# Latent input projections as 2x2 block products in Strassen's scheme, on one Trainium2 core

## The chip, the cores and the metric

The kernel runs on one core of a Trainium2 chip. The metric is the device time of one execution in microseconds (us); the number given for a kernel is the median of its runs. Engines are named as in the profile: PE is TensorE (PEld its weight loads), DVE is VectorE, ACT is ScalarE, POOL is GpSimd, SP is SyncE, whose queue issues the transfers.

## What is computed

One layer of a diffusion trunk for 128 context tokens and 1024 latent tokens of width 1024, all in float32. What matters here is the combined input projection, whose columns feed a pooling mixer, eight DeltaNet heads (q, k, v and gate, 128 columns each) and two merge gates:

```python
h = rmsnorm(x, norm1_g) * (1 + scale1) + shift1
proj = h @ w_in
a_out = pool_mixer(proj[..., OFF_POOL:OFF_Q], pool_w, pool_scale, grid) @ pool_proj
b_in, s_f, s_b = deltanet_mixer(proj, dn_conv, dn_a_log, dn_dt_bias, dn_onorm_g, s0_f, s0_b)
b_out = b_in @ dn_proj
merge = jax.nn.sigmoid(proj[..., OFF_MERGE:])
mixed = merge[..., :D_MODEL] * a_out + merge[..., D_MODEL:] * b_out
x = x + gate1 * (mixed @ w_out)
h = rmsnorm(x, norm2_g) * (1 + scale2) + shift2
x = x + gate2 * expert_choice_ffn(h, router_w, exp_w_gate, exp_w_up, exp_w_down)
```

`deltanet_mixer` applies a short convolution of five taps to q, k and v, normalises q and k, and runs a gated delta rule in chunks in both directions. `expert_choice_ffn` is a mixture of 16 experts; the change does not touch it.

## The kernel before, in words

The prologue computes the modulation, normalises and turns x into `hT3` (128 partitions x 8 steps of the contraction x 1152 tokens, context first) and makes q, k and v of head 0. Then a loop runs over heads 0 to 6 and a second copy of its body does head 7. After that come the merge of the branches, the output projection, the routing and the experts.

**Projections are the filling of the head loop.** A unit of work is one tile of 128 output columns over one span of tokens (span 0 is the 128 context tokens, spans 1 and 2 are 512 latent tokens each): `KD` = 8 matmuls that accumulate in one of PSUM banks 6 and 7, which alternate (`project`, L616). ACT copies each finished unit out (`evac_unit`, L647). One head's body projects q, k, v for the next head, the gate `g` of its own and two "side" tiles `A` and `B` of the merge and pooling columns, 18 units in the order `ORDER`; the last head does `g` and the side tiles A to F (`ORDER_LAST`). A unit may start when the unit two places before it has been copied out (`pj_drained`). The matmuls of the units are cut into pieces by the table `FILLS`, and `fill(place)` puts each piece between two dependent steps of the head's own work, so that PE has something to do while the others answer.

**The head's own work, in order of its places:** the norm of k ("nk", L765, which waits for ACT's silu and squares), q turned ("qT", L770), k and v turned (L779), the products kk and kq ("kk", L787). DVE multiplies kk with the decay table `dm` (L1085), which POOL has masked before (L1232), forms the first triangles (L1092, L1097), and PE turns them ("Y20" to "Y22", L794). Six levels double the size of the inverted blocks: products Z and P on PE (L802), copies on ACT (L976, L979), and on DVE nine predicated copies in each level (L1111, L1118, L1123) and one tap of the next head's convolution (L1053, L1055). Then "res", "fix" and the scan over nine chunks ("scan1a" to "scan8c"). POOL takes four differences and products of 1152 columns during the levels (L1247, L1250) and, when the scan has ended, adds and squares both directions' outputs (L1253, L1255); DVE and ACT normalise them (L1188, L1029, L1190), ACT does the silu of the gate (L1035), PE turns the result (L895), and DVE's last steps release the next head (`scan_done`). The fills "end1" and "end2" stand between the scan and that turning.

SP's queue, in the order of `head`: weights of q, v, k two heads on when `k2` is done, the next gate's weights, side tile A out and its next weights in, then the decay rows and states, side tile B out and its next weights in.

```python
ins = nc.tensor.matmul(unit_bank(order, name)[:, 0:n], w[:, k, :], hT3[:, k, at:at + n], start=(k == 0), stop=(k == KD - 1))
```

## Time and profile before

| | |
|---|---|
| median of 3 runs | 2492.16 us (2490.82 to 2493.74) |
| span of the profiled execution | 2491.1 us |
| around the span (median less span) | 1.1 us |
| PE, PEld busy | 96%, 70% of the span |
| DVE, ACT, POOL busy | 40%, 38%, 11% |
| one head of the loop | 140.6 us |
| matmuls of the projections (L616) | 925.2 us of 2401.1 us of PE |

An instruction of the profile has a line of the source, an engine, and the tiles it reads and writes; here nearly all tiles are views of one buffer, `arena`, so that lines tell more than names. A float32 matmul stands in the profile as two instructions. Durations of neighbouring matmuls overlap, so that a run of them is read from its start and end and not from the mean of one.

### The profile page before, as it was taken

The numbers are of one execution on the slowest core, as the hardware profiler recorded it, in microseconds if no ns is written. First come the engines' busy times: TensorE is split into PE (matmuls) and PEld (weight loads), VectorE is DVE, ScalarE is ACT, GpSimd is POOL, SyncE is SP. The second block draws the span as 40 slices with busy tenths as digits, with TensorE's granted clock in tenths as the row PEclk, the third lists the DMA queues.
The fourth block names the chain that finished last, engine by engine and source line by source line (L and its number), as shares of the span: only waits on it lengthen the run. The fifth ranks groups of instructions, "written<-read, shape, count | busy, mean of one in ns | idle before, by whom it ended". The sixth has DMA issues, their size and how long they took to land.

```text
span 2491.1 us, 39690 instructions
## 1 busy us (share of the span) xinstructions
PE 2401.1 (96%) x14448; PEld 1732.1 (70%) x14448; DVE 1007.9 (40%) x2061; ACT 938.0 (38%) x2447; POOL 285.9 (11%) x193
## 2 busy tenths in 40 slices
PE   6999999999999999999999999959999999999998
PEld 3466656566666656565644444649999999999996
DVE  2567575747556575744424524740001000100013
ACT  3164645556374655545421123212322232223213
POOL 0021221203111221201000000000101010101000
PEclk8999999999999999999999999979999999999999
DMA  9511212120201212021342422358886888688864
GB/s 335 221 48 37 68 37 68 26 79 1 76 29 37 68 37 68 1 78 37 107 178 106 146 75 93 119 178 279 287 298 232 288 286 299 230 287 287 299 230 160
DMA packets 198455, 361.94 MB, mean 145 GB/s; under 512 B 8954, under 2 KB 72327, under 8 KB 195243
## 3 DMA queue, kind: packets, MB, share of 16 engines
q1 hardware_dynamic: 192139, 341.77, 39.3%
q0 software_dynamic: 6176, 18.29, 2.9%
q8 instruction: 90, 1.47, 0.3%
q14 instruction: 50, 0.41, 0.1%
HBM read 319.97 MB, written 40.06 MB: 145 GB/s over the span
## 4 chain that ended last, share of the span: by engine, by line
PE 93%; DVE 2%; DMA 1%; issue 1%; ACT 1%; SPq 0%; DVEq 0%; POOL 0%; ACTq 0%; POOLq 0%
PE bank L616 32%; PE bank L2139 20%; PE bank L2153 10%; PE bank L1768 5%; PE bank L1505 4%; PE bank L802 3%; PE bank L1523 2%; PE bank L794 2%; PE bank L871 1%; PE bank L860 1%; PE bank L876 1%; PE bank L787 1%; DMA arena<-in_ada_w 1%; PE bank L851 1%; PE bank L875 1%
## 5 line engine op out<-in xcount | busy, mean ns | idle before, releaser
L616 PE MATMUL bank<-arena 128*128 128x512 f32 (+1 forms) x2496 | 925.2, 496 | 2.9 <-issue 1.2
L2139 PE MATMUL bank<-arena 128*128 128x144 f32 x4096 | 513.0, 286 | 3.0 <-ACT arena L2187 3.0
L2139 PEld LDWEIGHTS bank<-arena 128*128 128x128 f32 x4096 | 509.7, 190 | 3.2 <-ACT arena L2187 3.2
L616 PEld LDWEIGHTS bank<-arena 128*128 128x128 f32 x2496 | 374.6, 192 | 156.4 <-issue 154.0
L2254 DVE TENSOR_TENSOR arena<-arena,bank 128x144 f32<-128x144 f32 x128 | 39.2, 306 | 700.0 <-ACT arena L2201 700.0
L2153 PE MATMUL bank<-arena 128*128 128x144 f32 x2048 | 257.3, 286 | 0.7 <-DVE arena L2254 0.7
L2153 PEld LDWEIGHTS bank<-arena 128*128 128x128 f32 x2048 | 253.8, 190 | 1.9 <-DVE arena L2254 0.9
L802 PEld LDWEIGHTS bank<-arena 128*128 128x128 f16 x1296 | 98.3, 98 | 169.2 <-issue 156.1
L976 ACT ACTIVATE arena<-bank 128x384 f16<-128x384 f16 (+1 forms) x360 | 160.0, 495 | 140.1 <-PE bank L802 102.0
L2201 ACT ACTIVATE arena<-bank 128x144 f32<-128x144 f32 x128 | 37.4, 292 | 464.3 <-PE bank L2139 464.3
L647 ACT ACTIVATE arena<-bank 128x512 f32<-128x512 f32 (+1 forms) x156 | 76.6, 491 | 253.3 <-PE bank L616 253.0
L1055 DVE SCALAR_TENSOR_TENSOR arena<-arena 128x1156 f32<-128x1156 f32 x96 | 136.2, 1419 | 1.6 <-issue 1.3
L1768 PE MATMUL bank<-arena 128*128 128x512 f32 x288 | 128.7, 601 | 4.1 <-DVE arena L1662 2.1
L1111 DVE CAST_PREDICATED arena<-arena,bank 128x384 f16<-128x384 uint32 x144 | 79.8, 554 | 119.3 <-PE bank L802 119.1
L802 PE MATMUL bank<-arena 128*128 128x128 f16 x1296 | 123.7, 220 | 0.7 <-ACT arena L976 0.3
L1505 PE MATMUL bank<-arena 128*128 128x512 f32 x256 | 110.6, 592 | 1.3 <-DVE arena L1202 1.3
L1118 DVE COPY_PREDICATED arena<-arena 128x384 f16<-128x384 uint32 x144 | 101.1, 702 | 7.0 <-ACT arena L979 0.9
L1768 PEld LDWEIGHTS bank<-arena 128*128 128x128 f32 x288 | 53.9, 192 | 68.5 <-issue 66.3
L2208 ACT ACTIVATE arena<-bank,arena 128x128 f32<-128x128 f32 x128 | 47.2, 368 | 135.9 <-PE bank L2153 135.9
L1009 ACT ACTIVATE arena<-bank,arena 128x128 f32<-128x128 f32 x144 | 53.3, 370 | 106.1 <-PE bank L860 106.1
L1505 PEld LDWEIGHTS bank<-arena 128*128 128x128 f32 x256 | 48.4, 189 | 62.5 <-issue 60.9
L1168 DVE SCALAR_TENSOR_TENSOR arena<-arena,bank 128x128 f32<-128x128 f32 x128 | 44.7, 349 | 98.0 <-PE bank L876 98.0
(296 smaller groups left out, 2733.8 us busy)
## 6 DMA issues: line engine op xcount, KB each, us to landing
arena<-in_exp_w_gate SPq DMA_DIRECT2D x32, 2048.0 KB, 10.0
arena<-in_exp_w_up SPq DMA_DIRECT2D x32, 2048.0 KB, 15.0
arena<-in_exp_w_down SPq DMA_DIRECT2D x32, 2048.0 KB, 11.0
arena<-in_w_in SPq DMA_DIRECT2D x52, 512.0 KB, 5.3
arena<-in_ada_w SPq DMA_DIRECT2D x24, 1024.0 KB, 7.9
side_dram<-arena SPq DMA_DIRECT2D x20, 576.0 KB, 3.3
arena<-g_dram SPq DMA_DIRECT2D x16, 576.0 KB, 4.9
arena<-in_x_sample SPq DMA_DIRECT2D x16, 512.0 KB, 7.3
```

Of the source, the lines that this page charges most:

```text
L616: ins = nc.tensor.matmul(unit_bank(order, name)[:, 0:n], w[:, k, :], hT3[:, k, at:at + n], start=(k == 0), stop=(k == KD - 1))
L647: nc.scalar.activation(dst, bank[:, 0:n], ACT.Copy).then_inc(sem("pj_drained"), 1)
L802: last = nc.tensor.matmul(TRI[d][g][:, i * P:(i + 1) * P], lhs[:, 3 * g + i, :], rhs[:, 3 * g + i, :], start=(n == 0), stop=(n == len(term ...
L976: nc.scalar.activation(flat(dst, g), src[:, 0:384], ACT.Copy).then_inc(sem(f"drained{d}_act"), 1)
L1009: nc.scalar.activation(scan[:, 2, d, :], TRI[d][1][:, 0:P], ACT.Copy, scale=tab["kd"][:, ti, bass.ds(h + d * H, 1)])
L1055: ins = nc.vector.scalar_tensor_tensor(conv_to[j][:, 0:CW], raw[j][:, tap:tap + CW], w, conv_to[j][:, 0:CW], ALU.mult, ALU.add)
L1111: nc.vector.copy_predicated(up[:, 3 * g:3 * g + 3, :], masks[:, 0, lv + 1, :].unsqueeze(1).to_broadcast([P, 3, P]), TRI[1][g][:, 0:384].re ...
L1118: nc.vector.copy_predicated(low[:, 3 * g:3 * g + 3, :], rows, up[:, 3 * g:3 * g + 3, :]).then_inc(sem("low_changed"), 1)
L1505: last = nc.tensor.matmul(banks[n % RING][:, 0:CH], w_dn[half][:, k, col:col + P], bT3[:, k, CTX + c * CH:CTX + (c + 1) * CH], start=(k == ...
L1768: last = nc.tensor.matmul(banks[2 * (i % 2) + half][:, 0:512], mixT3[:, k, t * P:(t + 1) * P], w_outs[:, k, half * 512:(half + 1) * 512], ...
L2139: last = nc.tensor.matmul(banks[3 + f % 2][:, m * CAP:(m + 1) * CAP], w_unit[2 * half + m][:, k, col:col + P], xsT[:, k, :], start=(k == 0 ...
L2153: last = nc.tensor.matmul(banks[5 + dt % 2][:, 0:CAP], w_unit[4 + half][:, k, col:col + P], hid[:, k, :], start=(k == 0), stop=(k == KD - 1))
```

## The change

The latent tokens are two halves of 512 (`LH`), the contraction is two halves of 4 steps (`KH`), and the tiles of the loop are taken in pairs: (q,v), (k,g), (A,B), in the last head (A,B), (C,D), (E,F), with the last head's `g` alone. For a pair the latent part is a product of 2x2 blocks. It is done in seven block products of 4 matmuls of 512 columns, in place of eight; the jobs are called `1`, `2`, `6`, `7`, `5`, `4`, `3`, and the context units `c0` and `c1` go first. Four of the seven take sums of weight blocks or of blocks of x.

- The sums of x (three of 128x2048, and one in place over a block of `hT3`) are made once by POOL in the prologue. The last head's g2 therefore uses sums of weights too.
- The sums of weights (four of 128x512 for a pair, twelve in a head) are made by POOL in each head, in `sums_first` (two), `sums_third` and `sums_fourth`, the third once `c1` is done, the fourth once `2` is done.
- Jobs 6, 5, 3 accumulate on the bank of job 1, and 4 on that of job 7. Jobs `1`, `6`, `7`, `3` and the context are copied out by ACT, as many copies as before; jobs `2`, `5`, `4` are added to a result by DVE (`add_job`), nine adds of 128x512 from PSUM in a head, at places named by `add(place)`. A job waits for the copy or add of the job two before it, and the first job of a head for all of them.
- The table of pieces counts columns (`FILL`, units of 512) in place of matmuls. "start" has 5 units where it had 6 matmuls; "end1" has 4 where it had 6, "end2" 5 where it had 8.
- Side tiles A and B are both stored, and their next weights both loaded, after the head's last job. `w_dn` is loaded later; some buffers move, `attnT` shares `dm`.

```diff
+        PAIR_JOBS = ("c0", "c1", "1", "2", "6", "7", "5", "4", "3")
-        ORDER = ("q1", "q0", "v0", "k0", "g0", "A0", "B0", "q2", "v1", "v2", "k1", "k2", "g1", "g2", "A1", "A2", "B1", "B2")
-        ORDER_LAST = ("g1", "g0", "A0", "B0", "g2", "A1", "A2", "B1", "B2") + tuple(f"{x}{i}" for x in "CDEF" for i in range(3))
+        ORDER = pair_jobs("qv") + pair_jobs("kg") + pair_jobs("AB")
+        ORDER_LAST = pair_jobs("AB") + ("g0", "g1", "g2") + pair_jobs("CD") + pair_jobs("EF")
-        FILLS = {"start": 6, "nk": 5, "qT": 16, "kk": 16, "Y20": 8, "Y21": 8, "Y22": 2, "X0": 1, "X1": 1, "X2": 1, "res": 2, "fix": 4, "end1": 6}
+        UNIT = 512
+        FILL = {"start": 5, "nk": 2.75, "qT": 4, "kk": 4, "Y20": 1.5, "Y21": 1.5, "Y22": 1, "X0": 1, "X1": 1, "X2": 1, "res": 2, "fix": 3, "end1": 4}
+        def project(pe, h, order):
+            for i, job in enumerate(order):
+                bank = job_bank(order, job)
+                if i >= 2:
+                    bank_read(pe, h, order, order[i - 2])
+                elif order is not FIRST:
+                    pe.wait_ge(sem("pj_drained"), len(FIRST) + N_COPIES * h)
+                    pe.wait_ge(sem("pj_added"), 1 + N_SUMS * h)
...
+                else:
+                    one, two = weights_of(job[0]), weights_of(job[1])
+                    w, x = {"1": (one[:, 0:KH, :], h11), "2": (one[:, KH:KD, :], h21), "6": (w_sum[1], h_sum2), "7": (two[:, 0:KH, :], h_sum3),
+                            "5": (w_sum[0], h_sum1), "4": (two[:, KH:KD, :], h_sum4), "3": (one[:, KH:KD, :], h22)}[job[2]]
+                    if job[2] in "6573":
+                        pe.wait_ge(sem("sums_ready"), sums_before(h, order, job) + {"5": 1, "6": 2, "7": 3, "3": 4}[job[2]])
+                    for k in range(KH):
+                        ins = nc.tensor.matmul(bank[:, 0:LH], w[:, k, :], x[:, k, :], start=(k == 0 and job[2] in "127"), stop=(k == KH - 1), skip_group_check=(job[2] in "6543"))
...
+        def add_job(dve, h, order, job):
+
+            name, span, copied = {"2": (job[0], 1, "1"), "5": (job[1], 2, "7"), "4": (job[1], 1, "6")}[job[2]]
+            dve.wait_ge(sem("pj_drained"), copied_at(h, order, job[:2] + copied))
+            dve.wait_ge(sem("pj_filled"), job_at(h, order, job))
+            to = result(h, order, name, span)
+            nc.vector.tensor_tensor(to, to, job_bank(order, job)[:, 0:LH], ALU.add).then_inc(sem("pj_added"), 1)
...
+            def sums_first(pair, used):
+
+                n = sums_before(h, order, pair)
+                for name in pair:
+                    weights_wait(pool, h, order, name)
+                pool.wait_ge(sem("pj_filled"), used)
+                one, two = weights_of(pair[0]), weights_of(pair[1])
+                nc.gpsimd.tensor_tensor(w_sum[0], two[:, 0:KH, :], two[:, KH:KD, :], ALU.add).then_inc(sem("sums_ready"), 1)
+                summed(n + 1)
+                nc.gpsimd.tensor_tensor(w_sum[1], w_sum[0], one[:, 0:KH, :], ALU.subtract).then_inc(sem("sums_ready"), 1)
...
+            def sums_fourth(pair):
+
+                one = weights_of(pair[0])
+                pool.wait_ge(sem("pj_filled"), job_at(h, order, pair + "2"))
+                summed(sums_before(h, order, pair) + 2)
+                nc.gpsimd.tensor_tensor(one[:, KH:KD, :], one[:, KH:KD, :], w_sum[1], ALU.subtract).then_inc(sem("sums_ready"), 1)
...
+            first, second, third = ("AB", "CD", "EF") if last_h else ("qv", "kg", "AB")
+            pool.wait_ge(sem("scan_done"), h + 1)
+            sums_first(first, len(FIRST) + len(ORDER) * h)
+            sums_third(first)
+            sums_fourth(first)
```

In the rows below a line stands for its line in the kernel concerned: in the changed kernel L729 and L718 are the block and context matmuls, L1392 to L1407 the sums of weights, L1427 the masking of `dm` (L1232 before), L911 the products kk and kq (L787 before), L918 the turning for Y2 (L794 before).

**POOL, the loop's body from its start to the mask of Yf, before:**

```order
L1389 UNCONDITIONAL_BRANCH
L1389 ISA
L1232 ISA [waits decay_exp]
L1232 AFFINE_SELECT arena<-arena 128x1152
L1230 REGISTER_ALU
L1232 AFFINE_SELECT arena<-arena 128x1152 [waits decay_exp]
L1237 ISA
L1239 AFFINE_SELECT arena<-arena 128x384 [waits X_init] x6
```

and in the changed kernel:

```order
L1392 TENSOR_TENSOR arena<-arena 128x512 [waits pj_filled]
L1383 ISA
L1394 TENSOR_TENSOR arena<-arena 128x512 [waits sums_ready]
L1399 REGISTER_ALU
L1400 TENSOR_TENSOR arena<-arena 128x512 [waits pj_filled]
L1405 REGISTER_ALU
L1383 REGISTER_ALU [waits pj_filled]
L1407 TENSOR_TENSOR arena<-arena 128x512 [waits sums_ready]
L1425 ISA
L1427 ISA [waits decay_exp]
L1427 AFFINE_SELECT arena<-arena 128x1152
```

The four sums of the pair (q,v) stand ahead of the two masks of `dm`, and the last of them (L1407) waits for the job `2` of the pair.

**PE in the same body, from the end of kk and kq to the first turning for Y2, before:**

```order
L787 MATMUL bank<-arena 128x128 x2
L616 MATMUL bank<-arena 128x128 x5
L608 REGISTER_ALU
L614 REGISTER_ALU [waits w_in3]
L616 MATMUL bank<-arena 128x128 [waits pj_drained]
L616 MATMUL bank<-arena 128x128 x7
L614 REGISTER_ALU [waits w_side_in0]
L616 MATMUL bank<-arena 128x128 [waits pj_drained]
L616 MATMUL bank<-arena 128x128 x2
L807 ISA
L544 ISA [waits X_init]
```

and in the changed kernel, where the single L729 is the last matmul of job `qv2`, the next four are `qv6`, and the one that waits for `pj_added` is the first of `qv7`:

```order
L911 MATMUL bank<-arena 128x128 x2
L729 MATMUL bank<-arena 128x512
L668 REGISTER_ALU
L727 ISA [waits pj_drained]
L729 MATMUL bank<-arena 128x512 [waits sums_ready]
L729 MATMUL bank<-arena 128x512 x2
L931 ISA
L556 REGISTER_ALU [waits X_init]
...
L729 MATMUL bank<-arena 128x512
L666 REGISTER_ALU
L727 REGISTER_ALU [waits pj_added]
L729 MATMUL bank<-arena 128x512 [waits sums_ready]
```

The last matmul of `qv2` stands behind kk and kq, and `qv7` stands between the first and the second turning.

**SP, the last body's transfers between the head before it and its own, changed kernel:**

```order
L797 DMA arena<-g_dram 128x1152
L799 DMA arena<-in_state_dn_bwd 128x128
L788 DMA side_dram<-arena 128x1152 [waits pj_drained,pj_added]
L779 DMA arena<-in_w_in 128x8x128
L788 DMA side_dram<-arena 128x1152 [waits pj_drained,pj_added]
L779 DMA arena<-in_w_in 128x8x128
```

The last head begins with the pair (A,B), whose weights are the two L779; they are issued when the jobs of the head before have been copied and added. Before, the last head began with `g`, whose weights came much earlier.

## Rows read from the trace of the kernel before

**Rows 1.** The page: busy time of PE, and its granted clock in 40 slices.
```profile
PE 2401.1 (96%) x14448; PEld 1732.1 (70%) x14448; DVE 1007.9 (40%) x2061; ACT 938.0 (38%) x2447; POOL 285.9 (11%) x193
PEclk8999999999999999999999999979999999999999
```

**Rows 2.** Groups by line and shape, PE: busy us, mean ns; idle before.
```profile
L616 PE MATMUL bank<-arena 128*128 128x512 f32 x1664 | 821.4, 604 | 2.3 <-issue 1.2 <-ACT arena L287 1.0
```

**Rows 3.** The chain that ended last, in order of time: start us, us, what.
```profile
1098.96 12.88 PE bank L616 x30
...
1275.76 27.74 PE bank L1505 x64
```

**Rows 4.** Timeline of PE, head 1 to head 2: start us, us, engine, line.
```profile
395.55 13.04 PE L616 MATMUL bank<-arena 128*128 128x512 f32 x30
408.43 1.15 PE L895 MATMUL bank<-arena 128*128 128x128 f32 x9
...
414.91 2.10 PE L765 MATMUL bank<-arena 128*128 128x128 f32 x6
...
425.83 4.18 PE L787 MATMUL bank<-arena 128*128 128x128 f32 x36
429.85 3.74 PE L616 MATMUL bank<-arena 128*128 128x128 f32 x32
433.65 0.51 PE L794 MATMUL bank<-arena 128*128 128x128 f16 x6
...
442.03 0.34 PE L802 MATMUL bank<-arena 128*128 128x128 f16 x3
```

**Rows 5.** Timeline of POOL, same stretch.
```profile
426.95 2.37 POOL L1232 TENSOR_SCALAR_AFFINE_SELECT arena<-arena 128x1152 f32<-128x1152 f32 x2 [24.74 <-ACT arena L958]
```

**Rows 6.** Timeline of DVE: prologue's end, same stretch, merge.
```profile
128.10 0.06 DVE L1224 MEMSET arena<- 128x1 f32 x1
...
404.20 1.36 DVE L1190 TENSOR_TENSOR arena<-arena 128x1152 f32<-128x1152 f32 x1 [0.61 <-ACT arena L1031]
...
432.49 2.91 DVE L1097 COPY_PREDICATED arena<-arena 128x384 f16<-128x384 uint32 x6
...
1283.00 0.69 DVE L1564 TENSOR_TENSOR arena<-arena,bank 128x512 f32<-128x512 f32 x1 [1.99 <-PE bank L1505]
```

**Rows 7.** Timeline of ACT, same stretch.
```profile
405.48 1.26 ACT L1035 ACTIVATE arena<-arena 128x128 f32<-128x128 f32 x2
408.63 0.60 ACT L647 ACTIVATE arena<-bank 128x512 f32<-128x512 f32 x1 [1.89 <-PE bank L616]
...
416.69 1.52 ACT L935 ACTIVATE arena<-bank,arena 128x128 f32<-128x128 f32 x3
...
425.52 2.23 ACT L958 ACTIVATE arena<-arena 128x1152 f32<-128x1152 f32 x2
```

**Rows 8.** Windows: us, then busy of PE, PEld, DVE, ACT, POOL, clock, DMA.
```profile
416.69:422.88 6.19, 6.19 (x44) 5.07 (x43) 3.22 (x11) 6.09 (x26) 0.00 (x0) 1.00 0.00 0
```

**Rows 9.** Timeline of POOL, in the levels and in the last head.
```profile
339.30 3.73 POOL L1250 TENSOR_TENSOR arena<-arena 128x1152 f32<-128x1152 f32 x1 [4.01 <-DVE arena L1123]
...
1245.60 2.62 POOL L1253 TENSOR_TENSOR arena<-arena 128x1152 f32<-128x1152 f32 x1 [47.57 <-ACT arena L1015]
```

**Rows 10.** Timeline of DVE in the levels: predicated copies, alone and beside POOL.
```profile
309.51 0.56 DVE L1123 COPY_PREDICATED arena<-arena 128x384 f16<-128x384 uint32 x1
...
341.63 1.82 DVE L1118 COPY_PREDICATED arena<-arena 128x384 f16<-128x384 uint32 x1
```

**Rows 11.** Timeline of PE: behind a pause in the first head, and in the levels.
```profile
132.24 3.56 PE L765 MATMUL bank<-arena 128*128 128x128 f32 x6 [2.79 <-ACT arena L923]
...
310.75 0.33 PE L794 MATMUL bank<-arena 128*128 128x128 f16 x3
```

**Rows 12.** Windows, the same pause's end (columns as in rows 8).
```profile
132.00:134.00 2.00, 1.76 (x4) 1.27 (x5) 1.54 (x8) 2.00 (x5) 0.00 (x0) 0.50 1.16 295
```

**Rows 13.** Transfers of heads by tensor: queue, count, KB each, us to landing.
```profile
arena<-in_w_in SPq DMA_DIRECT2D x46, 512.0 KB, 5.1
```

More of the change, by code:

```diff
@@ L754, in body_pe @@
             order = ORDER_LAST if last_h else ORDER
-            side_work = projections(pe, h, order)
+            side_work = project(pe, h, order)
             def fill(place):
-                for _ in range(FILLS.get(place, UNITS_MAX * KD)):
-                    next(side_work, None)
+                for _ in range(steps_of(order, place)):
+                    next(side_work)
             fill("start")
@@ L907, in evac @@
             def evac(place):
-                for name in units_of(order, place):
-                    evac_unit(act, h, order, name)
+                for job in jobs_of(order, place):
+                    if not is_sum(job):
+                        copy_job(act, h, order, job)
             def silu(j):
@@ L1058, in body_dve, with add @@
         def body_dve(dve, h, last_h=False):
+            order = ORDER_LAST if last_h else ORDER
+            added = [0]
+            def add(place):
+                to = jobs_until(order, place)
+                for job in order[added[0]:to]:
+                    if is_sum(job):
+                        add_job(dve, h, order, job)
+                added[0] = to
             def decay_arguments(d):
@@ L1072, in body_dve @@
             decay_arguments(1)
+            add("qT")
             for g in range(3):
@@ L1150, in body_dve @@
             dve.wait_ge(sem("attn_ready"), 2 * h + 2)
+            add("fix")
             def remainder(t):
@@ L1179, in body_dve @@
             tap()
+            add("scan1b")
             state(1)
@@ L1183, in body_dve @@
                 tap()
+                add(f"scan{t}b")
                 state(t)
```

370 lines of the change are left out of this document (255 added, 115 removed).

## The prediction

> **What bounds the kernel now.** I read the page first: PE is busy for 96% of the span and its clock is granted in full nearly everywhere [rows 1]. The groups by line and shape then say what PE does: the 512-column matmuls of the projections alone are 821 us in 1664 instructions [rows 2]. The chain in order of time gives the pace: the fill behind the scan starts at 395.55 and again at 1098.96 us, five heads later, so a head takes 140.7 us [rows 3, 4], and within it PE hardly pauses. So fewer matmuls are worth their time, but only where the next dependent step is ready when PE arrives. That is a question for the timelines of the other engines. I count time in a head from 395.55 us, where the fill behind the last scan step begins [rows 4].
>
> **What the change takes off PE.** 30 instructions, that is 15 matmuls of 512 columns, last 12.88 us [rows 3, 4]: 0.86 us each. Each pair of tiles needs 28 in place of 32, and there are three pairs in each of eight heads: 96 matmuls, 82.4 us, 10.3 us a head. The context columns stay as many. This is the whole gain on offer. By the tables of pieces, of one head's 12 units (of 512 columns) 5 go behind the scan, 1.75 before kk, 4.25 among the turnings for Y2 and 1 at "fix"; none goes in the levels.
>
> **Behind the scan.** PE has 10 matmuls left in place of 15: 8.6 us. But the normalised output that the turning L895 needs is ready only when DVE's L1190 ends, at 404.20 + 1.36 = 405.56, that is 10.0 [rows 6]; before, PE came to it at 12.9 and was itself the last. So PE waits 1.4 us; L895 takes 1.2 to the next matmul (to 409.66), until 11.2. New: the next head's first job waits for the copy of job `AB3`, which ACT makes only after the silu of the gate, ended at 406.74, 11.2 [rows 7], 0.6 us more: 11.8. From the end of such a copy (409.23) to ACT's norms (416.69) are 7.5 us [rows 7]; so they come at 19.3, and with two context copies in front of them at 19.8, where it was 21.1. ACT is now the last here. Its work to the end of q's norm is 6.2 us less one copy of 0.5 [rows 8], then the copy of `qv1` (0.6) and the first of k turned (0.5): kk starts at 26.6, where it was 30.3 (425.83), and ends at 30.6 [rows 4]. So 3.7 us of the 5.8 that the smaller fills leave have been gained up to here.
>
> **The step that gives it back.** POOL's fourth sum stands ahead of the masks of `dm` and waits for job `2`, whose last matmul stands behind kk and kq: done at 31.5. A sum of 512 columns I price by POOL's add of 1152 alone, 2.62 us [rows 9]: 1.2 us. So the masks start at 32.8; they were at 426.95, 31.4 [rows 5]. From the mask to the first turning for Y2 (433.65) are 6.7 us of DVE and POOL [rows 4, 5]: 39.5, where it was 38.1. PE has `qv6` to do until 34.1 and then stands still for 5.4 us. Next, `qv7` needs the add of `qv2`, which DVE makes behind the six L1097: they end 1.75 us after the first turning starts [rows 4, 6], and the add, priced by a DVE product of 512 columns from PSUM, takes 0.69 [rows 6]. PE comes at 40.7 and waits until 41.9. Three of its matmuls and two turnings of 0.35 later, at 45.2, the levels begin; they began at 46.5 (442.03) [rows 4]. Of 9.5 us of matmuls saved up to here 1.3 are left.
>
> **The clock.** In the first head PE stood idle for 2.79 us, and the norm's matmuls behind it took 3.56 us at a granted clock of 0.50, the lower of its two levels (1.2 GHz), where they take 2.10 at the full one [rows 4, 11, 12]. 5.4 us idle will do the same: up to 1.5 us lost, of which the wait for the add hides half: 0.8. So the levels start 0.5 earlier than before.
>
> **The levels.** POOL's sums for (k,g) fall here. Beside POOL's product of 1152 a predicated copy of DVE lasts 1.82 us, alone 0.56, and POOL's product takes 3.73 where the add alone takes 2.62 [rows 9, 10]: they stop each other. And a copy that ends at 310.07 is turned by PE at 310.75, in the next level [rows 10, 11]: about 0.7 us of slack. Two sums back to back (behind `qv5`, in the first level) move DVE by up to 1.65 us: 1.15 lost; the third and fourth, one sum each, 0.65 and 0.8; the first two for (A,B) fall on the last copies before "res": 1.0. Together 3.6, less the matmul saved at "fix": 2.75. DVE's own adds fit into its waits. The bounds are nothing (each sum meets DVE in a wait) and the full 1.16 us for all eight sums from the levels on, 9.3 us. I take a value in the lower part, as each sum has slack in front of it. The Trainium skill, "SBUF — State Buffer", section "Who interferes with whom", says that a VectorE instruction with two SBUF inputs and a GpSimd one that reads SBUF exclude each other for a whole instruction; were none of it absorbed, the upper bound would hold. That is the fourth rival.
>
> **The scan.** The same columns, but "scan2b" has a context matmul of 128 where 512 stood, so that PE waits about 0.65 for ACT, and 0.2 for DVE's taps beside two sums: 0.85.
>
> **A head of the loop:** -1.3 + 0.8 + 2.75 + 0.85 = +3.1 us.
>
> **The ends.** The first fill must now wait for DVE's prologue (128.1 [rows 6], where PE had started at 124): with 4.5 us of jobs and about 1 us of delay by POOL's sums of x (4.7 us each by rows 9) its norm starts at 133.7, not 132.2 [rows 11]: +1.5, and 0.8 of clock. The last head had 10.6 units in front of Y2 and twice 4 in it, so there PE was the last; with masks, add and POOL's sums at the same distances its levels start at 48.6 in place of 61, then 8 more matmuls in the scan and 18 fewer behind it, and 2 us for sums, make it 9.9 us shorter from the scan of head 6 to L1505 (it lasted 1275.76 - 1098.96 = 176.8 [rows 3]). But its first job now needs the weights of A, issued after 11.8 and 5.1 us under way [rows 13], 0.4 for a store and issue ahead: 17.9, and B's at 18.8; this puts it back by 5.9, with 1.5 and 0.8 of clock: -1.7.
>
> **The sum:** 2.3 for the first front, six rounds from levels to levels 18.6, the rest of head 6 3.6, the last head -1.7: +22.8. The profiled execution took 2491.1 us of span and 1.1 around it, the median; so 2515 us.
>
> **Rivals.** (1) *PE stays the last everywhere* and the 82 us are gained, less the 5.9 of the last head: 2416. For it: PE's 96%. Against: L1190, the masks and the add have fixed distances that the removed fills covered. Chance 0.06. (2) *POOL's sums leave DVE alone*, since each falls into a wait. Then the levels give back nothing and a head is -1.3 + 0.8 - 0.86 + 0.65 = -0.7; with 2.3 for the front, -0.2 for the rest of head 6 and -3.7 for the last head the sum is -5.8: 2486, and 2479 if the clock stays full. DVE's waits of about 1 us in a level speak for it, the copy of 1.82 us against. Chance 0.17. (3) *The masks are not late*, the case on the other side. Masks that start when the first exponential of `dm` is done (28.5, L958 behind the copies of k [rows 7]) let Y2 turn at 35.3; PE waits 1.2 us only and keeps its clock, and the levels start 4.2 + 0.8 us sooner. A head is then -1.9 and eight of them take 40 us off my sum: 2475, with light sums as in (2) down to 2445. It decides from the point where job `2` ends before that exponential, 3 us earlier than I have it. Against it stands the order, with job `2` behind kk. Chance 0.15. (4) *DVE becomes the bound of the levels*: 9.3 us in place of 3.6, in eight heads +46: 2561. Chance 0.07. That the change doesn't do what it says I exclude for the matmuls; their number is fixed.
>
> **Numbers.** My case has 0.55. It reaches from 2500 to 2530, as each of the walk's nine waits may be off by some tenths and is taken seven times. Down to 2470 the range takes in rivals 2 and the greater part of 3; above it ends at 2535. Outside are 1 and 4 and a little of my own. 0.2%, about what a measurement of this kernel can tell, is 5 us. Faster by more: rivals 1, 3 and half of 2, 0.29; within: the rest of 2 and a little of mine, 0.13; slower: 0.58.
>
> **What would show it.** L729 and L718 together near 843 us in 2304 instructions. A pause of PE of about 5 us in front of L918 in each head, put down to DVE or POOL, and a clock below 1 there; L1407 of the first pair just ahead of L1427; a second pause before `qv7`; 1 to 2 us in front of L895's successor; predicated copies of DVE above 1 us more often than three times a head. I am wrong if PE reaches the levels more than 3 us earlier in a head than before (the masks did not count), or if the levels last 42 us as now (the sums did not count).

## The result, and the profile after

The changed kernel is slower: 2571.47 us (2571.28 to 2572.18, 4 runs) against 2492.95 us (2490.82 to 2494.79, 4 runs) on the same chip, a ratio of 1.0318 with a 95% interval of 1.0303 to 1.0333. The prediction was 2515 us with a range up to 2535: the sign was right, the size was not. The span of the profiled execution is 2569.5 us, 78.4 more than before.

The page of the changed kernel, busy time of the engines and PE's granted clock in 40 slices (before: [rows 1]):

```profile
PE 2370.0 (92%) x14256; PEld 1718.9 (67%) x14256; DVE 1122.5 (44%) x2133; ACT 943.5 (37%) x2447; POOL 440.5 (17%) x295
PEclk8989999999999999998999999979999999999999
```

PE is busy 31 us less and the kernel is 78 us longer, so PE now stands still for about 110 us more; DVE is busy for 115 us more and POOL for 155. The groups by line and shape (before: [rows 2]) show that the products are as few as intended, and, in the last column, new waits:

```profile
L729 PE MATMUL bank<-arena 128*128 128x512 f32 x1344 | 697.4, 622 | 21.6 <-ACT arena L763 21.6
L718 PE MATMUL bank<-arena 128*128 128x128 f32 x768 | 113.0, 298 | 16.3 <-DMA arena<-in_w_in 10.5 <-ACT arena L763 3.8 <-DVEq L1575 2.0
```

With the 69.8 us in 192 instructions of L710, the units outside a pair, the projections are 2304 instructions, the number that the prediction gave, but 880.2 us in place of its 843: 45 us less than before, not 82. That fits the clock: a 512-column instruction of L729 takes 622 ns on average where L616 took 604, and the mean granted clock of the execution is 0.968, where executions of the kernel before have 0.982 to 0.987.

One head of the loop in PE's timeline, from the fill behind the scan at 419.67 to the first products of the levels (L926) and on to the next fill. It is to be read against [rows 4]:

```profile
419.67 8.76 PE L729 MATMUL bank<-arena 128*128 128x512 f32 x20
429.75 1.20 PE L1019 MATMUL bank<-arena 128*128 128x128 f32 x9 [1.32 <-DVE arena L1343]
431.58 5.46 PE L718 MATMUL bank<-arena 128*128 128x128 f32 x32 [0.63 <-ACT arena L763]
439.15 1.12 PE L729 MATMUL bank<-arena 128*128 128x512 f32 x2 [2.11 <-ACT arena L763]
440.11 2.10 PE L889 MATMUL bank<-arena 128*128 128x128 f32 x6
442.05 1.88 PE L729 MATMUL bank<-arena 128*128 128x512 f32 x4
443.77 1.15 PE L894 MATMUL bank<-arena 128*128 128x128 f32 x9
444.75 3.60 PE L729 MATMUL bank<-arena 128*128 128x512 f32 x8
448.19 2.13 PE L903 MATMUL bank<-arena 128*128 128x128 f32 x18
450.15 4.18 PE L911 MATMUL bank<-arena 128*128 128x128 f32 x36
454.17 3.60 PE L729 MATMUL bank<-arena 128*128 128x512 f32 x8
463.36 0.82 PE L918 MATMUL bank<-arena 128*128 128x128 f16 x6 [5.59 <-DVE arena L1242]
463.97 3.93 PE L729 MATMUL bank<-arena 128*128 128x512 f32 x4
...
471.03 0.33 PE L926 MATMUL bank<-arena 128*128 128x128 f16 x3
...
569.21 8.76 PE L729 MATMUL bank<-arena 128*128 128x512 f32 x20
```

The head lasts 149.54 us where it lasted 140.6. Two pauses stand out: 2.11 us ahead of job `1`, which waits for ACT, and 5.59 us ahead of the first turning for Y2 (L918). From 439.15 to 457.7 PE does not pause at all.

The same places, read from the starts of these rows in each kernel, are used from here on. The times are us from the start of the fill behind the scan, the mean of the six rounds that lie within the loop; "scan" is the first matmul of the scan with the inverted blocks (L984 in the changed kernel), and the last column is the length of a head:

| kernel | norm (L889) | kk (L911) | Y2 (L918) | levels (L926) | scan | next fill |
|---|---|---|---|---|---|---|
| before | 19.5 | 30.4 | 38.2 | 46.6 | 102.05 | 140.6 |
| changed | 20.8 | 31.3 | 44.5 | 51.9 | 110.8 | 150.1 |
| fourth sum behind the masks | 20.75 | 31.45 | 40.4 | 46.3 | 105.1 | 144.5 |
| copy of c0 early | 16.7 | 26.8 | 40.0 | 46.9 | 105.8 | 145.1 |
| both | 16.7 | 26.8 | 35.7 | 41.6 | 100.5 | 139.8 |
| thin sums in the levels | 20.8 | 31.3 | 44.5 | 52.0 | 107.4 | 146.75 |
| thin adds | 21.0 | 31.6 | 44.8 | 52.0 | 110.8 | 150.2 |
| sums in quarters | 20.9 | 32.3 | 45.95 | 53.2 | 110.2 | 149.5 |
| before, less matmuls | 16.3 | 28.3 | 36.1 | 41.1 | 95.7 | 134.2 |
| five moves | 16.7 | 26.8 | 35.7 | 40.3 | 99.15 | 138.4 |
| and quarters | 16.7 | 26.8 | 35.6 | 40.25 | 97.2 | 136.5 |

POOL and ACT in that head name what is late. POOL's timeline (before: [rows 5]):

```profile
437.12 1.33 POOL L1400 TENSOR_TENSOR arena<-arena 128x512 f32<-128x512 f32 x1 [1.33 <-PE bank L718]
455.36 1.27 POOL L1407 TENSOR_TENSOR arena<-arena 128x512 f32<-128x512 f32 x1 [16.90 <-PE bank L729]
456.66 2.37 POOL L1427 TENSOR_SCALAR_AFFINE_SELECT arena<-arena 128x1152 f32<-128x1152 f32 x2
```

ACT's timeline, ahead of the norm (before: [rows 7]):

```profile
435.12 2.39 ACT L1040 ACTIVATE arena<-arena 128x128 f32<-128x128 f32 x4
437.52 1.28 ACT L1054 ACT_TABLE_LOAD   x1
438.82 0.45 ACT L763 ACTIVATE arena<-bank 128x128 f32<-128x128 f32 x2
```

The fourth sum (L1407) ends 0.03 us before the masks (L1427) start, and it has waited for job `2`, as the prediction had it. What the prediction had not seen is the last row: the copies of the two context jobs stand on ACT behind six silus (four of them in the first row) and a table load, although PE had c0 ready near 434, half way through its 32 context matmuls.

### The profile page after: what moved, and what is told of

It is laid out like the page before. It is cut to its first block, busy times and chain, and to the rows that moved or that the text cites. A ratio compares the mean times of both kernels' runs of the same rounds, so it can differ in the third digit from the quotient of the medians.

```text
span 2569.5 us, 39903 instructions
## 1 busy us (share of the span) xinstructions
PE 2370.0 (92%) x14256; PEld 1718.9 (67%) x14256; DVE 1122.5 (44%) x2133; ACT 943.5 (37%) x2447; POOL 440.5 (17%) x295
## 4 chain that ended last, share of the span: by engine, by line
PE 52%; DVE 2%; issue 1%; DMA 1%; ACT 1%; POOL 0%; SPq 0%; DVEq 0%; ACTq 0%; POOLq 0%
PE bank L2373 20%; PE bank L2387 10%; PE bank L2002 5%; PE bank L1739 4%; PE bank L729 3%; PE bank L1757 2%; PE bank L710 1%; PE bank L2011 1%; PE bank L2345 1%; PE bank L2355 1%; PE bank L926 0%; PE bank L718 0%; DMA arena<-in_w_in 0%; PE bank L2413 0%; PE bank L995 0%
## 5 line engine op out<-in xcount | busy, mean ns | idle before, releaser
L729 PE MATMUL bank<-arena 128*128 128x512 f32 x1344 | 697.4, 622 | 21.6 <-ACT arena L763 21.6
L2373 PEld LDWEIGHTS bank<-arena 128*128 128x128 f32 x4096 | 509.6, 190 | 3.2 <-ACT arena L2421 3.2
L729 PEld LDWEIGHTS bank<-arena 128*128 128x128 f32 x1344 | 221.9, 195 | 119.4 <-issue 95.0
L2387 PEld LDWEIGHTS bank<-arena 128*128 128x128 f32 x2048 | 253.8, 189 | 1.9 <-DVE arena L2488 0.9
L926 PEld LDWEIGHTS bank<-arena 128*128 128x128 f16 x1296 | 98.7, 98 | 149.8 <-issue 127.4
L1186 DVE SCALAR_TENSOR_TENSOR arena<-arena 128x1156 f32<-128x1156 f32 x96 | 143.1, 1490 | 0.3
L918 PE MATMUL bank<-arena 128*128 128x128 f16 x648 | 72.7, 233 | 70.8 <-DVE arena L1242 44.4
L2002 PE MATMUL bank<-arena 128*128 128x512 f32 x288 | 128.7, 601 | 4.1 <-DVE arena L1896 2.1
L718 PE MATMUL bank<-arena 128*128 128x128 f32 x768 | 113.0, 298 | 16.3 <-DMA arena<-in_w_in 10.5
L918 PEld LDWEIGHTS bank<-arena 128*128 128x128 f16 x648 | 46.5, 104 | 119.7 <-issue 65.7
L926 PE MATMUL bank<-arena 128*128 128x128 f16 x1296 | 123.5, 219 | 0.0
L718 PEld LDWEIGHTS bank<-arena 128*128 128x128 f32 x768 | 104.3, 210 | 26.3 <-issue 26.3
L763 ACT ACTIVATE arena<-bank 128x128 f32<-128x128 f32 (+1 forms) x156 | 76.1, 493 | 106.7 <-PE bank L710 48.0
L1264 DVE COPY_PREDICATED arena<-arena 128x384 f16<-128x384 uint32 x144 | 111.8, 776 | 6.8 <-DVE arena L1257 0.9
L1134 ACT ACTIVATE arena<-bank,arena 128x128 f32<-128x128 f32 x144 | 53.3, 370 | 165.0 <-PE bank L984 165.0
L1739 PE MATMUL bank<-arena 128*128 128x512 f32 x256 | 110.6, 592 | 1.3 <-DVE arena L1356 1.3
L1257 DVE CAST_PREDICATED arena<-arena,bank 128x384 f16<-128x384 uint32 x144 | 79.6, 552 | 65.9 <-PE bank L926 64.0
## 6 DMA issues: line engine op xcount, KB each, us to landing
arena<-in_exp_w_gate SPq DMA_DIRECT2D x32, 2048.0 KB, 10.1
```

The lines of the kernel that those rows point to most:

```text
L718: ins = nc.tensor.matmul(bank[:, 0:CTX], weights_of(name)[:, k, :], hT3[:, k, 0:CTX], start=(k == 0), stop=(k == KD - 1))
L729: ins = nc.tensor.matmul(bank[:, 0:LH], w[:, k, :], x[:, k, :], start=(k == 0 and job[2] in "127"), stop=(k == KH - 1), skip_group_check=( ...
L918: last = nc.tensor.transpose(TRI[d][g].bitcast(F16)[:, i * P:(i + 1) * P], src[:, 3 * g + i, :], ident_h)
L926: last = nc.tensor.matmul(TRI[d][g][:, i * P:(i + 1) * P], lhs[:, 3 * g + i, :], rhs[:, 3 * g + i, :], start=(n == 0), stop=(n == len(term ...
L1186: ins = nc.vector.scalar_tensor_tensor(conv_to[j][:, 0:CW], raw[j][:, tap:tap + CW], w, conv_to[j][:, 0:CW], ALU.mult, ALU.add)
L1257: nc.vector.copy_predicated(up[:, 3 * g:3 * g + 3, :], masks[:, 0, lv + 1, :].unsqueeze(1).to_broadcast([P, 3, P]), TRI[1][g][:, 0:384].re ...
```

## The experiments

A ratio is to the kernel before on the same chip as the experiment. The medians of that kernel there were 2493.24 to 2495.27 us, against 2492.95 beside the changed kernel, so differences to the changed kernel's 2571.47 us are good to about 2 us.

### The two pauses, each taken away alone

The first edit lets POOL make the fourth sum behind the masks of `dm` (and, in the last head, lets the gate's sums wait for it, not shown):

```diff
             sums_third(first)
-            sums_fourth(first)
             for d in range(2):
...
                 nc.gpsimd.affine_select(out=dm[d], in_=dm[d], ...)
+            sums_fourth(first)
```

> The changed kernel with one step moved: POOL makes the fourth sum of the first pair behind the two masks of dm and not ahead of them. Theory A (the masks are the step that is late, and the sum is what makes them late): the changed kernel's masks start 1.3 us behind job 2 (456.66 us), its first exponential of dm ends near 451, so DVE's first product with dm starts when PE's kk and ACT's exponential are there, near 452.6 in place of 458.0; Y2 turns 5.4 us earlier, PE's 5.6 us pause in front of it goes to under 0.5, and the stretch at a clock of 0.5 behind it (2.2 us lost) goes too, while the add of qv2 holds qv7 up by about 0.9. That is 5.4 to 7.4 us in each of eight heads: 2512 to 2528 us. Theory B (something else ahead of the levels is last, DVE's adds or the copies of ACT): at most the 1.3 us of one sum a head, 2561 or more.

Measured: 2531.51 us (2522.48 to 2540.09), 40 less than the changed kernel; ratio to before 1.0156 (1.0120 to 1.0191). From kk to Y2 it takes 8.9 us in place of 13.2, and the levels begin 5.9 us behind Y2 in place of 7.4. Theory A holds in kind, 3.5 us outside its numbers: Y2 comes 4.3 us sooner behind kk, not 5.4. DVE shows why. In one of its heads, kk being at 440.84:

```profile
443.31 2.88 DVE L1230 SCALAR_TENSOR_TENSOR arena<-bank,arena 128x384 f32<-128x384 f32 x6
446.10 2.57 DVE L1237 TENSOR_TENSOR arena<-arena 128x384 f16<-128x384 f32 x3
```

The three L1237 take 2.57 us where they took 1.49 in the changed kernel, because the moved sum runs at 446.05, beside them. The spread of 18 us has a likely cause of its own, told in the last section.

The second edit puts ACT's copy of c0 between the squares of k and the silu of q:

```diff
             silu(1)
+            act.wait_ge(sem("scan_done"), h + 1)
+            copy_job(act, h, order, order[0])
             silu(0)
             silu(2)
             act.preload_act_table_set(LN_EXP)
-            act.wait_ge(sem("scan_done"), h + 1)
-            evac("start")
+            for job in jobs_of(order, "start")[1:]:
+                copy_job(act, h, order, job)
```

> The changed kernel with ACT's copy of the first job (qvc0) put between the squares of k and the silu of q, in place of behind all six silus and the table load. Theory A (in front of the norm PE waits 2.1 us for that copy, and from the norm to kk PE is itself the last, so what is late there stays late): PE starts the norm of k 2.1 us sooner in each head, kk, the masks and Y2 follow by the same 2.1 us; 4 us in the first head; 2551 to 2556 us. Theory B (the pause is harmless, as ACT's norms and the transposes set the time of kk, as the prediction had it): under 0.7 us a head, 2566 or more.

Measured: 2540.22 us (2535.37 to 2541.23), 31 less; ratio to before 1.0183 (1.0166 to 1.0200). Theory A was right in kind but foresaw only half of the size: kk comes 4.5 us earlier, not 2.1. Its PE timeline:

```profile
420.12 3.83 PE L718 MATMUL bank<-arena 128*128 128x128 f32 x32 [0.63 <-ACT arena L763]
423.97 1.13 PE L729 MATMUL bank<-arena 128*128 128x512 f32 x2
424.93 2.10 PE L889 MATMUL bank<-arena 128*128 128x128 f32 x6
```

The 32 context matmuls take 3.83 us and not 5.46: the clock is full here. In the changed kernel some heads also have the 3.83 us, but there the time only made the pause for the copy longer (3.74 in place of 2.11).

Both edits together:

> The changed kernel with both moves: POOL's fourth sum of the first pair behind the masks, and ACT's copy of the first job in front of the silu of q. Theory A (two pauses of PE one behind the other, each on the path): the norm of k at 16.7 us of a head, kk 10.0 behind it, Y2 8.9 behind kk, the levels 5.9 behind that, the scan 58.9 and the next head 39.3 further: 139.8 us a head, where the changed kernel has 149.5 to 150.7; the last head like that of the first move alone. 2490 us. Theory B (the pauses overlap, so that the second move gives only what the first has left): 2515 us or more. A third possibility: the stretch of low clock behind a pause falls on the norm and the turnings in some heads, as with the first move alone, 2.9 us in each such head: 2493 to 2510.

Measured: 2495.22 us (2493.76 to 2498.93, 10 runs), ratio to before 1.0008 (0.9998 to 1.0018), no difference that can be measured. A head lasts 139.77 us, within 0.1 of theory A, though the whole is 5 us above its 2490; the low clock on the norm, by which the third possibility reached such times, is in none of the six rounds. So two places in the order of ACT and POOL made the whole loss against the kernel before, 76 us. In a round the edits gave 5.7 and 5.0 us one by one and 10.35 together, so they nearly add up. The medians gave 40 and 31; the first lies between two groups of runs 16 us apart, so that the 5 us missing to 76 say nothing.

### Sums and adds in the levels

Sums behind the first pair of a head were made of 1 column of each step, then all of DVE's adds of 1 column:

```diff
+                c = P if pair == first else 1
-                nc.gpsimd.tensor_tensor(w_sum[0], two[:, 0:KH, :], two[:, KH:KD, :], ALU.add).then_inc(sem("sums_ready"), 1)
+                nc.gpsimd.tensor_tensor(w_sum[0][:, :, 0:c], two[:, 0:KH, 0:c], two[:, KH:KD, 0:c], ALU.add).then_inc(sem("sums_ready"), 1)
...
```

```diff
-            nc.vector.tensor_tensor(to, to, job_bank(order, job)[:, 0:LH], ALU.add).then_inc(sem("pj_added"), 1)
+            nc.vector.tensor_tensor(to[:, 0:1], to[:, 0:1], job_bank(order, job)[:, 0:1], ALU.add).then_inc(sem("pj_added"), 1)
```

> The changed kernel with all sums of weights behind the first pair of a head made of 1 column in each of the four steps, where they have 128 (the products that use them are then not those of the reference). Theory A (POOL's sums and DVE's predicated copies keep each other out in the levels): the stretch from the first Z to the scan goes from 58.4 us to 54 or 55, 3.4 to 4.3 us a head of the loop, about 2541 to 2547 us. Theory B (the levels are longer because DVE also has nine adds to make): the stretch stays above 57.5 us, 2565 or more.

> The changed kernel with each of DVE's nine adds of a head made of 1 column where it has 512 (q, k, v, the gate and the side tiles are then not those of the reference). Theory A (the adds fall into DVE's waits, or behind Y2 where PE waits for one): under 1 us a head, 2563 to 2571 us. Theory B (the adds, 0.69 us each, stand on DVE's path in the levels and in the scan): 3 to 4 us a head, 2540 to 2547 us.

Measured: 2547.66 us (2545.85 to 2549.45) with thin sums, 2569.59 (2568.39 to 2572.10) with thin adds. The levels last 55.4 and 58.9 us, where the changed kernel has 58.9 and the kernel before 55.45. So the sums cost 3.4 us there, as much as the levels had grown, and the nine adds cost nothing there. The groups of DVE over the levels of one head, changed kernel (us busy, mean ns):

```profile
L1264 DVE COPY_PREDICATED arena<-arena 128x384 f16<-128x384 uint32 x18 | 14.4, 798 | 0.9 <-DVE arena L1257 0.2
L1269 DVE COPY_PREDICATED arena<-arena 128x384 f16<-128x384 uint32 x18 | 13.1, 728 | 0.9
L1257 DVE CAST_PREDICATED arena<-arena,bank 128x384 f16<-128x384 uint32 x18 | 9.9, 552 | 7.9 <-PE bank L926 7.9
L1186 DVE SCALAR_TENSOR_TENSOR arena<-arena 128x1156 f32<-128x1156 f32 x4 | 6.7, 1668 | 0.0
```

and with thin sums:

```profile
L1264 DVE COPY_PREDICATED arena<-arena 128x384 f16<-128x384 uint32 x18 | 13.3, 738 | 0.9 <-DVE arena L1257 0.2
L1269 DVE COPY_PREDICATED arena<-arena 128x384 f16<-128x384 uint32 x18 | 10.0, 558 | 0.9
L1257 DVE CAST_PREDICATED arena<-arena,bank 128x384 f16<-128x384 uint32 x18 | 9.9, 553 | 7.9 <-PE bank L926 7.9
L1186 DVE SCALAR_TENSOR_TENSOR arena<-arena 128x1156 f32<-128x1156 f32 x4 | 5.7, 1420 | 0.0
```

The predicated copies and taps with all inputs in SBUF lose 5.2 us to the sums (34.2 against 29.0), of which 3.4 are on the path; the one whose data come from PSUM (L1257) takes 552 ns beside a sum or not (all 144 of them 546 to 561 ns, one at 478.43 us in the middle of a sum that runs from 478.17 to 479.65). The Trainium skill, "SBUF — State Buffer", section "Who interferes with whom", has it so: outside the two-port modes a VectorE instruction with at most one SBUF input does not contend with GpSimd, while one with two contends with a GpSimd instruction that reads SBUF, over ports that only one of them holds at a time. The trace agrees, by the 552 ns on the one side and the 34.2 us against 29.0 on the other.

If a stall is as long as POOL's instruction, shorter instructions should help. Each sum as four:

```diff
+            def by_steps(out, one, two, op):
+                for k in range(KH):
+                    last = nc.gpsimd.tensor_tensor(out[:, k, :], one[:, k, :], two[:, k, :], op)
+                last.then_inc(sem("sums_ready"), 1)
...
-                nc.gpsimd.tensor_tensor(w_sum[0], two[:, 0:KH, :], two[:, KH:KD, :], ALU.add).then_inc(sem("sums_ready"), 1)
+                by_steps(w_sum[0], two[:, 0:KH, :], two[:, KH:KD, :], ALU.add)
```

> The changed kernel with each of the twelve sums of a head made by four instructions of 128 columns in place of one of 512. Theory A (POOL and DVE keep each other out for one whole instruction, so a shorter one of POOL holds a predicated copy up for less): the levels go from 58.9 us down to between 56 and 57.5; 2550 to 2562 us, if the four instructions take about as long as the one. Theory B (the two share in proportion to the time that POOL reads, whatever the length of its instructions): the levels stay at 58.9 or grow by the cost of more instructions; 2570 to 2590.

Measured: 2560.70 us (2558.88 to 2561.72), 11 less than the changed kernel, ratio to before 1.0268 (1.0251 to 1.0285). The levels last 57.0 us, as theory A has it. (kk is later here by the low clock, which more of the heads have, and Y2 by the fourth sum, whose four instructions stand ahead of the masks.) The predicated copies beside the first two sums of (k,g) took 1.63 and 1.17 us in the changed kernel; here three take 0.82, 0.76 and 0.81. That is so although POOL now needs 4.73 us for two sums that took some 2.9:

```profile
474.98 4.73 POOL L1387 TENSOR_TENSOR arena<-arena 128x128 f32<-128x128 f32 x8 [6.08 <-PE bank L729]
```

### Fewer matmuls and nothing else

In the kernel before, steps of the units were left out at about the places of the change:

```diff
+        SKIP = {"nk": 1, "qT": 3, "kk": 6, "Y20": 5, "Y21": 5, "Y22": 1, "fix": 1, "end1": 5}
+        SKIP_LAST = {"nk": 1, "kk": 2, "Y20": 2, "Y21": 1, "fix": 1, "end1": 5}
...
                 for k in range(KD):
+                    if order is not FIRST and 0 < k < KD - 1 and to_skip[0] > 0:
+                        to_skip[0] -= 1
+                        yield
+                        continue
```

> The kernel before with about as much matmul time left out as the change removes, at about the places where the change removes it (5 matmuls of 512 behind the scan, 1 and 3 of 128 before kk, 16 of 128 and 1 of 512 around Y2, 1 of 512 in fix; in the last head 12 of 512): 9.9 us a head, some 80 in all, and neither sums nor adds. Those units then lack one of eight steps. Theory A (the loss comes from the sums, the copies' place and the masks, and the saved time by itself is mostly worth having): the turning of o 2.8 us earlier, kk about 4, the levels 6.8 and the end of the head 7.6: 133 us a head, 2431 us, within 12. Theory B (PE is last everywhere): 80 us less, 2413. Theory C (the head is bound by the fixed chain of ACT, POOL and DVE, so that fewer matmuls give almost nothing even without the sums): 2475 to 2490.

Measured: 2441.21 us (2439.72 to 2442.21), ratio to before 0.9787 (0.9771 to 0.9804). The rounds give 6.4 us each of 9.9, 52 us of some 80 in all, inside theory A's range. Even with nothing added, then, a third of the saved time is lost: PE waits 1.3 us for DVE ahead of the turning of o, twice 1.1 us for ACT's copies ahead of kk, and 1.4 us for DVE ahead of Y2.

### What beats both

Three more moves on top of the two: DVE's add of `qv2` behind the first pair of L1242, the matmul of "scan8b" moved to the end of the head, and g0, g1 ahead of the pair (A,B) in the last head:

```diff
+                if g == 0:
+                    add("kk")
...
+        FILL[f"scan{NT - 1}b"] = 0
...
-        ORDER_LAST = pair_jobs("AB") + ("g0", "g1", "g2") + pair_jobs("CD") + pair_jobs("EF")
+        ORDER_LAST = ("g0", "g1") + pair_jobs("AB") + ("g2",) + pair_jobs("CD") + pair_jobs("EF")
```

> The two moves, and three more: DVE's add of qv2 stands behind the first pair of its six predicated copies for Y2, not behind all six; the matmul at scan8b goes to the end of the head, where PE waits 1.3 us; the last head begins with g0 and g1 and then takes the pair (A,B), whose weights come late. Theory A (each move takes away a wait of PE that is on the path): 1.05 us for the add in eight heads, 0.86 for the matmul in seven, about 5 for the last head, 19 us below the kernel with the two moves: 2471 us. Theory B (what is moved only turns up as the next wait): within 5 us of the kernel with the two moves, 2485 to 2495.

Measured: 2481.47 us (2478.85 to 2482.09), ratio to before 0.9946 (0.9929 to 0.9962), between the two theories. The rounds are 1.4 us shorter than with two moves: 1.3 from Y2 to the levels, so the add was on the path, but 0.1 in and behind the scan. The matmul at "scan8b" only made room for a wait of 0.5 for ACT. From the last scan of the loop to L1739's stage (L1745 here) it is 175.6 us, where it was 177.5: the weights of A are covered now, but PE waits ahead of Y2 for masks that stand behind the sums of that pair:

```profile
1129.91 0.39 PE L919 MATMUL bank<-arena 128*128 128x128 f16 x2 [6.97 <-DVE arena L1245]
```

Next come the quarters on top, with all four sums of the last head's first pair behind the masks; then the first sums of the third pair put off until the scan has begun:

```diff
+            for d in range(2):
+                pool.wait_ge(sem(f"vn_filled{d}"), h * NT + 1)
             sums_first(third, job_at(h, order, second + "5"))
```

> The kernel with the five moves, and two more edits: every sum of weights in four instructions of 128 columns, and in the last head all four sums of the first pair behind the masks (there three of them still stand ahead and wait for weights and for job c1, and PE stands still for 7.0 us in front of Y2). Theory A (both act as in the kernels where they were seen alone): the levels from 58.9 to 57.0 us in seven heads and 1.6 less in the last, 15 us, and 6 of the 7.0 us of the pause, 2460 us. Theory B (shorter stalls of DVE are only taken by the next wait, now that PE comes to the levels earlier, and the last head's pause goes to its levels): above 2473.

> The same, and the first two sums of the third pair wait until the scan has begun, where before they fell on the last predicated copies of the levels. Theory A (a sum costs only where DVE's copies are the last): without any sum and with as many matmuls the levels took 54.6, with quarters 57.0; two of the six sums that fall there should be worth 0.6 to 0.8 us a head, and in the scan, where DVE has waits of its own, they cost 0.1 to 0.3: 4 to 5 us below the kernel with the quarters. Theory B (in the scan they hold up DVE's remainder and state, each on the path, as much): no difference within 2 us, or slower.

Measured for the first: 2457.51 us (2455.99 to 2457.96), ratio to before 0.9858 (0.9841 to 0.9874), as theory A has it (the pause ahead of Y2 in the last head is 1.5 us, from 7.0). For the second: 2456.49 (2455.71 to 2457.79), ratio 0.9855 (0.9839 to 0.9872), where theory A fails. The levels last 57.0 us in both, and the stretch from the scan to the next fill 39.2. Sums at the very end of the levels cost nothing there.

Two more edits on the kernel with the quarters, one matmul moved from "qT" to "kk", and eight instructions for a sum:

```diff
-        FILL = {"start": 5, "nk": 2.75, "qT": 4, "kk": 4, ...
+        FILL = {"start": 5, "nk": 2.75, "qT": 3, "kk": 5, ...
```

> The fastest kernel so far but one (five moves, quarters, the last head's sums behind the masks) with one matmul of 512 fewer between the norm and kk and one more between kk and Y2. Theory A (from the norm to kk PE is itself the last, and from kk to Y2 DVE is): norm to kk from 10.04 to 9.18 us, kk to Y2 stays 8.9 with PE's pause there going from 1.3 to 0.4: 0.86 us a head, 2450 to 2452 us. Theory B (ACT's and DVE's chain for q and k, not PE, sets kk): kk comes no earlier and PE only waits in front of it; 2456 to 2459.

> The kernel with the quarters, with every sum of weights in eight instructions of 64 columns. Theory A (a stall of DVE is as long as one instruction of POOL): the stalls halve again and the levels come from 57.0 down to about 56; 2449 to 2453 us. Theory B (POOL's cost for each instruction makes eight of them read for longer than they save): the levels stay at 57.0 or grow, 2457 to 2466.

Measured: 2458.14 us (2456.43 to 2458.92) and 2457.40 (2455.68 to 2459.53), neither different from 2457.51. With the matmul moved, kk comes 0.66 us earlier and Y2 0.2 later. DVE tells what is last then:

```profile
423.06 2.88 DVE L1233 SCALAR_TENSOR_TENSOR arena<-bank,arena 128x384 f32<-128x384 f32 x6 [1.01 <-POOL arena L1438]
```

It waits for the masks, these for ACT's exponential. From the norm to Y2 the paths over PE and over ACT are equally long within 0.7 us, and theory A named only one. The time is the one that theory B gave, but not for its reason, as kk did come earlier. With eighths the levels stay at 57.0, and two sums take POOL 6.07 us: theory B holds, shorter instructions bring nothing from here on. What holds the remaining 2.4 us over the 54.6 of the kernel with fewer matmuls was not settled; thin sums left 0.8 of them.

## Why the prediction was wrong, step by step

The walk of the prediction had four terms, in all 22.8 us. The stage behind the heads starts at 1353.20 us in place of 1275.76, 77.4 later [rows 3]:

| stretch | predicted | measured |
|---|---|---|
| start, up to the levels of head 0 | +2.3 | +10.0 |
| six rounds from levels to levels | 6 x 3.1 = +18.6 | 6 x 9.5 = +57.0 |
| rest of head 6 | +3.6 | +4.2 |
| last head | -1.7 | +6.3 |

Of the 56 us between 2515 and 2571.47, 54.6 lie in these rows; 1.0 more fell behind the heads, and the time around the span was 1.8 us, not 1.1.

- **What the change takes off PE:** right in the number of matmuls, and 0.86 us each at the full clock. The sign "L729 and L718 together near 843 us in 2304 instructions" left out L710; with it the 2304 are there, but 880.2 us.
- **Behind the scan:** right up to the first job. PE turns o 10.1 us behind the start of the fill (10.0 predicted) and starts the first job at 11.9 (11.8).
- **The step that failed** is the next sentence: "they come at 19.3, and with two context copies in front of them at 19.8", and with it "kk starts at 26.6". It counted the two copies as 0.5 us of ACT's time and made ACT the last up to kk. But job `1` may start only when c0 has been copied, that copy stands behind six silus and a table load, and the norm stands behind job `1` on PE's own queue. PE pauses for 2.1 to 3.7 us, the norm comes at 20.8, and from there PE needs 10.0 us of its own work to kk at the full clock, a path that the prediction did not walk at all. kk came at 31.3; with the copy moved it came at 26.76. That this is nearly the predicted 26.6 is in part luck: ACT's norms came at 19.5 then (19.8 predicted), but PE was the last at kk, which came at 26.1 once PE had one matmul less ahead of it. The late kk is 4.7 us of the 6.4 by which a round was missed, and the same pause, 4.03 us at the start, put the first norm at 139.1 in place of 133.7, 5.4 of the 7.7 missed there.
- **The step that gives it back:** right in kind. The fourth sum took 1.27 us (1.2), masks and Y2 came 6.5 and 13.2 us behind kk (6.2 and 12.9), PE paused for 5.6 (5.4). The wait of `qv7` for its add did not show, as the matmul ahead of it ran at the low clock; it showed as 1.05 us, with the fourth sum moved, once that was gone.
- **The clock:** the term was 0.8 and too small by 0.9. Behind the pause PE ran at 1.2 GHz for 4.3 us, and Y2 to the levels took 7.4 on average where the fast kernels need 4.6 to 5.9. The windows of the changed kernel (clock is the third number from the end):

```profile
463.36:467.70 4.34, 4.34 (x11) 1.72 (x12) 4.34 (x8) 1.88 (x4) 2.37 (x3) 0.50 0.00 2
```

- **The levels:** 3.4 us in place of 2.75, near the value that was taken in the lower part of 0 to 9.3. Rivals 2 and 4, nothing and everything, both fall: the levels cost neither nothing nor 9.3 us.
- **The scan:** about 0.75 against 0.85.
- **The last head:** its first job waited 6.43 us for weights and started at 17.7 (17.9 predicted), and the stretch behind the scan is 15.5 us shorter, as 18 matmuls make. Its levels began at 58.9 where the terms gave 56.8: kk came at 34.8 where they gave 34.0, and from Y2 to the levels it took 11.2 us in place of 9.9. In both stretches PE ran at the low clock for longer than the terms of 1.5 and 0.8 allow: behind the first pause it was granted 0.56, so that 32 context matmuls took 6.39 us in place of 3.83, and behind the second 0.51 for 6.3 us. And nobody had looked for the weights of E, loaded only when the last job of (C,D) is done, in the scan:

```profile
1187.60 6.39 PE L718 MATMUL bank<-arena 128*128 128x128 f32 x32 [6.43 <-DMA arena<-in_w_in]
...
1309.90 3.33 PE L718 MATMUL bank<-arena 128*128 128x128 f32 x14 [4.09 <-DMA arena<-in_w_in]
```

These are 2.1 and 4.1 of the 8.0 us missed; the other 1.8 were not separated.
- **Rivals 1 and 3:** PE was not last everywhere (even without sums only 52 of 80 us came), and the masks were late. The range failed because each side of it came from the costs that the walk named, and none stood for a wait that it had overlooked and that came back in every head. Neither of its two signs of being wrong came either, for both looked for a smaller loss or for none: the levels began 5.3 us later than before in a head, not 3 earlier, and grew.

## What to carry to other kernels

When a job queue is cut finer or reordered, look for every job that waits for the copy of the one two before it, and find that copy in the order of the engine that makes it: what counts is what stands ahead of it there, not how long it takes. Walk each engine's own work between two milestones, PE's too, even where another engine was last so far. Here the fewer products were a gain of 1.4% once one of ACT's copies, one of POOL's sums, one of DVE's adds and the order of the last head had been moved and the sums cut into short instructions, and a loss of 3.2% before.

## What the runs showed of the hardware that was not expected

**A pause costs clock at a place that varies from head to head.** In the profiled execution of the changed kernel the heads alternate between two forms, with the same two pauses of PE (1.3 and 0.6 us) in front. In one, the 32 context matmuls run at a mean clock of 0.69 (5.46 us) and the norm at 1.00. In the other they run at the full clock (3.83 us), PE then waits 3.7 us in place of 2.1 for the same copy, and the instructions of job `1` and the first part of the norm run at 0.50:

```profile
581.12 3.83 PE L718 MATMUL bank<-arena 128*128 128x128 f32 x32 [0.63 <-ACT arena L763]
588.69 1.94 PE L729 MATMUL bank<-arena 128*128 128x512 f32 x2 [3.74 <-ACT arena L763]
590.43 3.02 PE L889 MATMUL bank<-arena 128*128 128x128 f32 x6
```

In windows, from the changed kernel:

```profile
431.58:437.04 5.46, 5.46 (x32) 5.27 (x32) 3.73 (x13) 5.42 (x9) 2.55 (x2) 0.69 0.79 224
...
589.50:592.00 2.50, 2.50 (x6) 1.39 (x5) 0.00 (x0) 0.37 (x1) 0.00 (x0) 0.50 0.53 206
```

The first form's low clock is hidden by the wait for the copy; the second's is on the path, and kk comes at 32.1 to 32.2 in place of 30.5. With only the masks' step moved, two of six rounds lasted 146.4 us and four 143.49, 2.9 apart: in the two the whole norm takes 4.05 us. That is the likely reason why its runs lie at 2522 to 2524 and 2539 to 2540 us; it is not shown, as only one of the faster was profiled, and the slower would need the long form in nearly every head. With both moves that pause is gone, all six rounds are within 0.1 us, and ten runs lie within 5.2 us.

**Four short instructions of POOL cost more than one long one, and the path was shorter nevertheless.** The fourth sum, which no DVE instruction disturbs, took 1.70 us in four of 128 columns and 1.27 in one of 512, 1.3 times as long. In the levels, beside DVE, two sums took 4.73 us in eight against some 2.9 in two, 1.65 times. DVE's stalls beside them were shorter, and the levels with them by 1.9 us.
